# Moving the low weight halves of a split fp32 matmul to other byte offsets in each ring slot

## What is computed

```python
D_MODEL, SEQ, D_FF, D_FF_2 = 1024, 256, 2816, 4096

def swiglu(h, w_gu, w_down):
    gate, up = jnp.split(h @ w_gu, 2, axis=-1)
    return (jax.nn.silu(gate) * up) @ w_down

def first_block(x, ...):
    for i in range(2):
        x = x + 0.5 * swiglu(rms_norm(x, norm_ffn1[i]), w_ffn1_gu[i], w_ffn1_down[i])
        h = rms_norm(x, norm_mix[i])
        x = x + (stick_breaking_attention(h, ...) if i == 0 else multiscale_pool_mixer(h, ...))
        x = x + 0.5 * swiglu(rms_norm(x, norm_ffn2[i]), w_ffn2_gu[i], w_ffn2_down[i])
        gate = jax.nn.sigmoid(rms_norm(x, norm_ple[i]) @ w_ple_gate[i])
        x = x + gate * (p[i] @ w_ple_proj[i])

def second_block(x, ...):
    for i in range(2):
        m = nsa_mixer(h, ...) if i == 0 else fox_mixer(h, ...)      # h = rms_norm(x)
        x = x + rms_norm(m)
        x = x + rms_norm(jnp.square(jax.nn.relu(rms_norm(x) @ w_up[i])) @ w_down[i])
```

## Time and profile before

| | |
|---|---|
| Time, three executions | 1667.28 us median (1666.3 to 1668.62) |
| Span of the profiled execution | 1666.6 us |
| TensorE busy with matmuls | 1631.1 us, 98% |
| Weight loads (beside the matmuls) | 1444.1 us, 87% |
| VectorE, ScalarE, GpSimd busy | 62%, 49%, 9% |
| HBM read | 280 MB, 169 GB/s over the span |
| Mean granted TensorE clock | 0.997 |

### The profile page before, as it was taken

The page is one execution under the profiler, slowest core; times in us unless marked ns, Lnnn a source line. Parts: engine busy times, 40 slices in busy tenths (PEclk is TensorE's granted clock), DMA queues, the critical chain, the costliest instruction groups (busy, mean ns, idle before and its releaser), DMA issues.

```text
span 1666.6 us, 25696 instructions
## 1 busy us (share of the span) xinstructions
PE 1631.1 (98%) x10390; PEld 1444.1 (87%) x10390; DVE 1031.5 (62%) x1060; ACT 810.0 (49%) x999; POOL 148.9 (9%) x117
## 2 busy tenths in 40 slices
PE   8999999999999999999999999988999999999998
PEld 7888887888889888888888998756998999889987
DVE  6454667755457645568454588766755578566554
ACT  6343567544345534456443566344544465454442
POOL 2000123300002100011000131211000000000000
PEclk9999999999999999999999999999999999999999
DMA  8545452364553554555454353412454535335551
GB/s 306 215 161 201 153 190 76 130 252 159 201 199 127 208 203 169 202 200 197 177 195 183 137 204 127 152 51 77 167 188 177 194 134 203 127 127 193 186 179 49
DMA packets 41212, 282.19 MB, mean 169 GB/s; under 512 B 4592, under 2 KB 4720, under 8 KB 7728
## 3 DMA queue, kind: packets, MB, share of 16 engines
q1 hardware_dynamic: 40752, 279.60, 45.6%
q0 software_dynamic: 384, 1.51, 0.2%
HBM read 280.04 MB, written 1.05 MB: 169 GB/s over the span
## 4 chain that ended last, share of the span: by engine, by line
PE 88%; DVE 5%; ACT 3%; issue 1%; POOL 1%; DMA 1%; POOLq 0%; DVEq 0%; SPq 0%; ACTq 0%
PE ps L373 28%; PE ps L376 27%; PE ps L377 27%; DVE w_lo L1722 2%; PE ps L576 1%; ACT arena L1556 1%; POOL arena L2469 1%; ACT arena L1554 0%; DMA raw<-weights 0%; PE ps L679 0%; PE ps L502 0%; DVE stat L2163 0%; ACT arena L1566 0%; DVE X L1882 0%; POOL arena L2492 0%
## 5 line engine op out<-in xcount | busy, mean ns | idle before, releaser
L1722 DVE TENSOR_TENSOR w_lo<-raw,w_hi 128x2048 fp32r<-128x2048 f32 x261 | 594.8, 2298 | 150.3 <-ACT w_hi L1245 150.1
L1245 ACT ACTIVATE w_hi<-raw 128x2048 fp32r<-128x2048 f32 x261 | 491.2, 1907 | 47.7 <-DMA raw<-weights 45.7
L373 PE MATMUL ps<-w_hi,hT_hi 128*128 128x512 f32 (+1 forms) x984 | 384.0, 390 | 10.6 <-DVE hT_lo L1749 7.0
L377 PE MATMUL ps<-w_hi,hT_lo 128*128 128x512 f32 (+1 forms) x984 | 375.2, 381 | 0.0
L376 PE MATMUL ps<-w_lo,hT_hi 128*128 128x512 f32 (+1 forms) x984 | 374.7, 381 | 0.0
L373 PE MATMUL ps<-hT_hi,w_hi 128*128 128x256 f32 x984 | 283.4, 288 | 1.3 <-DVE hT_lo L1749 1.2
L376 PE MATMUL ps<-hT_lo,w_hi 128*128 128x256 f32 x984 | 278.2, 283 | 0.0
L377 PE MATMUL ps<-hT_hi,w_lo 128*128 128x256 f32 x984 | 278.2, 283 | 0.0
L373 PEld LDWEIGHTS ps<-w_hi,hT_hi 128*128 128x128 f32 x984 | 186.2, 189 | 45.4 <-DVE w_lo L1737 7.0
L377 PEld LDWEIGHTS ps<-w_hi,hT_lo 128*128 128x128 f32 x984 | 185.9, 189 | 36.1
L376 PEld LDWEIGHTS ps<-w_lo,hT_hi 128*128 128x128 f32 x984 | 186.5, 190 | 32.0 <-issue 0.7
(11 more groups left out here) (269 smaller groups left out, 1818.2 us busy)
## 6 DMA issues: line engine op xcount, KB each, us to landing
raw<-weights SPq DMA_DIRECT2D x261, 1024.0 KB, 4.8
raw<-weights SPq DMA_DIRECT2D x12, 256.0 KB, 7.1
X<-x SPq DMA_DIRECT2D x4, 256.0 KB, 6.2
out<-X SPq DMA_DIRECT2D x4, 256.0 KB, 2.1
arena<-p POOLq DMA_DIRECT2D x2, 256.0 KB, 5.8
arena<-counts POOLq DMA_DIRECT2D x1, 512.0 KB, 5.0
arena<-nsa_tables POOLq DMA_DIRECT2D x1, 448.0 KB, 6.1
const<-constants SPq DMA_DIRECT2D x1, 427.0 KB, 7.5
```

The source lines that it names most:

```text
L373: mm = nc.tensor.matmul(dst, a_hi, b_hi, start=start, stop=False, skip_group_check=True)
L377: return nc.tensor.matmul(dst, a_lo, b_hi, start=False, stop=stop, skip_group_check=True)
L1245: nc.scalar.activation(unit_cols(w_hi, u, 0, UNIT), raw[:, r * UNIT:(r + 1) * UNIT], ACT.Copy).then_inc(hi_done.sem, 1)
L1722: nc.vector.tensor_tensor(unit_cols(w_lo, u, 0, UNIT), raw[:, r * UNIT:(r + 1) * UNIT], f(unit_cols(w_hi, u, 0, UNIT)), ALU.subtract).then ...
```

## The change

Each slot of the two weight rings becomes 2,064 columns apart (`SLOT`), 64 bytes more than the 2,048 that it holds. Within its slot, the low half begins 0, 16, 32, 48, 64 or 96 bytes further, by slot (`LO_SHIFT` in columns of 4 bytes). `H_SHIFT` is 0 and moves nothing. To make room, `ones` and `ones_neg` become single columns, read with a step of 0 by `broadcast_to`. The number and the order of the instructions on every engine stay as they were; only addresses change, and the size of one load: `const` has 254 columns less (600 in place of 854, 300 KB in place of 427 KB).

```diff
 UNIT = 2048
 RAW, RING = 3, 6
+SLOT = UNIT + 16
+LO_SHIFT = (0, 4, 8, 12, 16, 24)
+H_SHIFT = 0
...
-for _name, _n in [("ident", P), ("after_neg", P), ("ones_neg", P), ("ones", P),
+for _name, _n in [("ident", P), ("after_neg", P), ("ones_neg", 1), ("ones", 1),
...
-        w_hi, w_lo = sb("w_hi", RING * UNIT, f32r), sb("w_lo", RING * UNIT, f32r)
+        w_hi, w_lo = sb("w_hi", RING * SLOT, f32r), sb("w_lo", RING * SLOT + 16, f32r)
...
-        hT_hi, hT_lo = sb("hT_hi", KC * TOKENS, f32r), sb("hT_lo", KC * TOKENS, f32r)
+        hT_hi, hT_lo = sb("hT_hi", KC * TOKENS + H_SHIFT, f32r), sb("hT_lo", KC * TOKENS, f32r)
...
         def unit_cols(t, u, a, n):
-            s = (u % RING) * UNIT
+            s = (u % RING) * SLOT + (LO_SHIFT[u % RING] if t is w_lo else 0)
             return t[:, s + a:s + a + n]
...
-  mm = nc.tensor.matmul(bank(7, tok * P, P), at(SQUARES + tok * P, P), K("ones"), ...)
+  mm = nc.tensor.matmul(bank(7, tok * P, P), at(SQUARES + tok * P, P), K("ones").broadcast_to((P, P)), ...)
...
-  nc.tensor.matmul(A(0, s, P, P), K("ones_neg"), nB[:, s * P:(s + 1) * P], ...)
+  nc.tensor.matmul(A(0, s, P, P), K("ones_neg").broadcast_to((P, P)), nB[:, s * P:(s + 1) * P], ...)
```

More of the change, by code:

```diff
@@ L501, in sums @@
                 for tok in range(TT):
-                    mm = nc.tensor.matmul(bank(7, tok * P, P), at(SQUARES + tok * P, P), K("ones"), start=tok == 0, stop=True, skip_group_check=True)
+                    mm = nc.tensor.matmul(bank(7, tok * P, P), at(SQUARES + tok * P, P), K("ones").broadcast_to((P, P)), start=tok == 0, stop=True, skip_group_check=True)
                 mm.then_inc(sums_full.sem, 1)
@@ L680, in after @@
                         for s in (2 * b, 2 * b + 1):
-                            nc.tensor.matmul(A(0, s, P, P), K("ones_neg"), nB[:, s * P:(s + 1) * P], start=False, stop=True, skip_group_check=True)
+                            nc.tensor.matmul(A(0, s, P, P), K("ones_neg").broadcast_to((P, P)), nB[:, s * P:(s + 1) * P], start=False, stop=True, skip_group_check=True)
                     nc.tensor.matmul(bank(2), K("after_neg"), nB, start=True, stop=True).then_inc(after_full.sem, 1)
@@ L2070, in fox @@
                 step(nc.vector.scalar_tensor_tensor(LOGF, LOGF, 0.0, LOG1P, ALU.min, ALU.subtract))
-                nc.vector.tensor_tensor_scan(MINUS_C, K("ones")[:, 0:1].broadcast_to((P, TOKENS)), LOGF, 0.0, ALU.mult, ALU.subtract).then_inc(c_ready.sem, 1)
+                nc.vector.tensor_tensor_scan(MINUS_C, K("ones").broadcast_to((P, TOKENS)), LOGF, 0.0, ALU.mult, ALU.subtract).then_inc(c_ready.sem, 1)
                 dve.wait_ge(*c_ready.due(me))
@@ L2607, in constants @@
     put("after_neg", -(i[:, None] > i[None, :]).astype(np.float32))
-    put("ones_neg", -np.ones((P, P)))
-    put("ones", np.ones((P, P)))
+    put("ones_neg", -np.ones((P, 1)))
+    put("ones", np.ones((P, 1)))
     put("mask", np.concatenate([np.zeros((P, P)), np.where(i[None, :] <= i[:, None], 0.0, NEG)], axis=1))
```

## The result

The changed kernel takes 1671.31 us (median of 20 runs, 1669.31 to 1672.84), the kernel before 1667.78 us (20 runs, 1666.05 to 1669.11). The ratio is 1.002, 95% interval 1.0014 to 1.0027: slower by 3.5 us. The profiled execution has a span of 1667.7 us against 1666.6. The forecast was 1669.8 us.

What follows compares the result with a forecast made beforehand. The prediction took TensorE's own stream, busy 98%, as the bound. Its terms, +6.4 - 4.1 + 1.0 - 0.8 = +2.5 us, put the span at 1669.1 and the forecast time at 1669.8 us, range 1655 to 1684.

Steps and rivals of the forecast that it cites:

- the likeliest case, mixed with both signs: Matmul triples: some forms slower, others faster, +2.5 us in sum, 1669.8 us (1664 to 1675); chance 0.36.
- TensorE's stream is the bound, and addresses set its pitch: Whole kernel: TensorE busy 98% of the span; addresses matter only by setting its pitch or slowing a loader beyond its cover.
- The 32 bytes of hid_lo are the cause of the difference between the forms over hT and hid: Triples using hid_lo: its 32-byte offset makes 256-column triples 9 ns shorter and 512-column triples 19 ns longer.
- 512 columns over hT, +6.4 us: Weights moving over hT, slots 1 to 5, 676 triples: half of a possible 19 ns loss each, +6.4 us.
- 256 columns of hT and the 96 others, -4.1 us: 912 triples in slots 1 to 5: half of a possible 9 ns gain each, -4.1 us.
- 256 columns of hid, +1.0 us: 744 triples of hid over weights: already in the faster loose rhythm, could only lose by returning to 120.0 ns; +1.0 us.
- slots 2 and 5 come to the same offset modulo 64; if that restores the lock: 256 columns of hid, 232 triples: low halves meeting hid_lo's offset might restore the 120.0 ns rhythm, costing 9 ns, +2.1 us.
- 512 columns over hid, -0.8 us: Weights moving over hid, 80 triples in slots 2 and 5: equal offsets could give back 19 ns; -0.8 us taken.
- High halves against hT and hid, 0 in the sum: High halves in even slots, 64 bytes from activations modulo 128: adds to the range only, 0 to the sum.
- second rival: Only the 256-column forms react, offsets loosening the rhythm over hT: -9.7 us, 1657.6 us; chance 0.27.
- the third: 512 columns over hT slow down as over hid, +12.8 us, +2.1 from hid, nothing back at 256: 1682 us; chance 0.22.
- the fourth: Nothing changes: the ports don't meet and the hT and hid difference has another cause; 1667.3 us; chance 0.15.

## Why the prediction came out as it did

The time was inside the range, 1.5 us above the forecast, and the likeliest case, mixed with both signs, is what happened. That the forecast came so close is in part luck: the largest misses, +3.3 us on 512 columns over hT and -4.1 on 256 columns of hT, nearly cancel. Step by step:

- *TensorE's stream is the bound, and addresses set its pitch.* Right. The loaders, the broadcast ones and the smaller load cost nothing, as priced.
- *The 32 bytes of hid_lo are the cause of the difference between the forms over hT and hid.* Right, and shown by the run that removed them.
- *512 columns over hT, +6.4 us.* Measured +9.7. The half price was taken for 676 triples with a shifted low half; in fact all 888 changed, by 10.9 ns, since slot 0 changed as well.
- *256 columns of hT and the 96 others, -4.1 us.* Measured -8.2. The same mistake: 912 triples at half of 9 ns, where all 1,080 changed by 7.6 ns on average.
- *256 columns of hid, +1.0 us.* Measured +2.8. The step "slots 2 and 5 come to the same offset modulo 64; if that restores the lock" failed: modulo 256 these low halves stand at 32 and `hid_lo` at 96, and the slots are at 353.5 ns. The dearest is slot 1 (359.6). Its mean is that of the lock, but its pitches are not (117.7, 120.7 and 121.2 ns).
- *512 columns over hid, -0.8 us.* Measured -1.1, and again not for the reason given: the cheap slots are 1 and 3 (687.7, 688.0), not 2 and 5.
- *High halves against hT and hid, 0 in the sum.* This is the step that failed, and with it the reading of places modulo 64 and 128 bytes. The distance of the slots alone gives 1.8 of the 2.0 thousandths, part of it from low halves that the longer ring puts 128 bytes from their high halves, and the activations 64 bytes further give +7.8 us by themselves. The 0 was off by little only because its two large parts, +8.3 and -7.5 us in the run with the slots alone, nearly cancel.

The second rival (only 256 columns react), the third (512 columns lose, nothing comes back at 256) and the fourth (nothing changes) are out by the table of forms. For the fourth the prediction named the Trainium skill, "SBUF — State Buffer", section "Who interferes with whom", by which TensorE has two independent read ports and never waits on anyone. If that is taken to mean that offsets change nothing, the traces disagree: 64 bytes of distance make 17 ns in 683. Nor do multiples of 16 bytes leave the pitch alone: hT 16 bytes off takes 695.2 ns in place of 683.3. Why a common place modulo 256 bytes gives 120.0 and 226.7 ns, and why the forms answer with opposite signs, no run here settles. That the weight load of the next matmul and the moving stream of the present one meet in SBUF is one reading; it is not shown. Nor was a run made in which all operands move together, so it stays open whether only the distances between them count.

## What to carry to other kernels

Before pricing an address change, read the pitch of each matmul form from the starts, not the busy times, and look for one operand in the trace that already stands elsewhere: here `hid_lo` was a ready experiment that gave sign and size. A change that shifts everything at once can lose on one form what it gains on another and end at nearly no change; place operands by form instead (here 10.8 us, 0.64%). A tensor that grows moves everything allocated behind it, so write out the places of all operands for each version, modulo more than one grid: two expectations above went by places that their kernels did not have. And take slots whose own shift was 0 as a control: if they move too, the priced cause is not the whole one.

## What the runs showed of the hardware

- The pitch of these fp32r matmuls depends on where moving and stationary operands lie modulo 256 bytes. All at the same place: 226.7 ns for 512 columns and 120.0 for 256. Off it, in nearly all stages, a triple of 512 columns takes 687 to 702 ns in place of 680, and one of 256 columns 341 to 360 in place of 360. For 512 columns 8 bytes already act (692.0 ns).
- It is mostly enough that one of the four operands of a triple is off, but not always (226.7 ns with hT_lo 16 bytes off in one stage, 696.8 ns a triple in another), and the rhythm also depends on what ran just before.
- VectorE's subtraction and ScalarE's copy kept 2298 and 1908 ns with their two inputs and the output at unlike places, and a moving operand read with step 0 took the same 275 ns as a full one.
